# The time mixer's three sums by ones as two products of split operands, the variance sum behind ten weight groups, and affines and state scalings on ScalarE

## The reference, cut to what matters

```python
decay = exp(-DECAY_SCALE * sigmoid(w0 + tanh(wl) @ w_w2))
a = sigmoid(a0 + al @ w_a2)
kk = heads(k * k_k)
kk = kk / maximum(norm(kk, axis=-1), 1e-12)             # sum 1: squares over a head
k = k * (1.0 + (a - 1.0) * k_a)
y = rwkv7_scan(r_h, w_h, k_h, v_h, kk, a_h)
ym = mean(y, axis=-1)
yv = mean(square(y - ym), axis=-1)                      # sum 3: variance over a head
y = (y - ym) * rsqrt(yv + GN_EPS) * gn_g + gn_b
bonus = sum(r_h * k_h * r_k, axis=-1) * v_h             # sum 2
y = (y + bonus) * g
```

## Time and profile before

| | |
|---|---|
| median of 3 runs | 2407.47 us (2406.66 to 2407.55) |
| profiled execution, first to last instruction | 2404.5 us |
| PE busy | 2157.6 us, 90% |
| DVE busy | 1529.0 us, 64% |
| ACT busy | 684.3 us, 28% |
| software DMA queue (gathers) | 53.1% of 16 engines' span |

### The profile page before, as it was taken

How to read it: one execution, slowest core, us unless ns; L and a number is a source line. 1 busy time by engine, 2 the same in 40 slices (tenths; PEclk the granted TensorE clock), 3 DMA queues, 4 the chain that set the end, 5 groups by cost and what they waited for, 6 DMA issues and landing times.

```text
span 2404.5 us, 37848 instructions
## 1 busy us (share of the span) xinstructions
PE 2157.6 (90%) x15331; PEld 1510.5 (63%) x15331; DVE 1529.0 (64%) x2605; ACT 684.3 (28%) x1366; POOL 659.7 (27%) x539
## 2 busy tenths in 40 slices
PE   9999999999999999998999889978877787777776
PEld 8999999999899999987554444433332233222222
DVE  7778888888765455548876567667446444444445
ACT  6555555455344444432121111111011000000000
POOL 1000000000000000004554555555455445444442
PEclk9999999999999999999999999999999999999999
DMA  6533333333367666679999999999999999999997
GB/s 213 141 95 98 102 88 101 103 88 98 106 184 194 185 187 187 190 270 342 417 427 424 425 423 426 427 427 426 427 427 428 426 427 427 427 427 427 427 427 289
DMA packets 348320, 708.19 MB, mean 295 GB/s; under 512 B 13834, under 2 KB 272482, under 8 KB 281826
## 3 DMA queue, kind: packets, MB, share of 16 engines
q0 software_dynamic: 74176, 537.01, 53.1%
q1 hardware_dynamic: 273732, 168.55, 24.1%
q10 hardware_dynamic: 240, 0.22, 0.0%
HBM read 703.63 MB, written 2.10 MB: 294 GB/s over the span
## 4 chain that ended last, share of the span: by engine, by line
DMA 36%; PE 17%; issue 2%; DVE 2%; POOL 1%; DVEq 0%; ACT 0%; POOLq 0%; ACTq 0%
DMA query_w<-in_v_table,experts 17%; DMA rows<-in_v_table,experts 13%; PE bank L1980 7%; PE project L1980 4%; DMA rows<-in_u_table,experts 3%; DMA up_rows<-in_u_table,experts 3%; PE bank L247 2%; DMA down_row_more<-in_v_table,experts 2%; PE bank L1896 2%; PE project L247 1%; PE bank L1938 0%; PE bank L1944 0%; PE bank L1612 0%; PE bank L1923 0%; POOL rows L1851 0%
## 5 line engine op out<-in xcount | busy, mean ns | idle before, releaser
L2102 DVE CUSTOM_DVE_ANT_0 rows<-rows,h 128x2048 f32<-128x2048 f32 x170 | 388.7, 2292 | 329.7 <-DMA rows<-in_u_table,experts 329.5
L1851 POOL DMA_INDIRECT rows<-in_u_table,experts x170 | 182.9, 1076 | 1097.7 <-DVE experts L1449 1040.0
L232 DVE TENSOR_TENSOR w_half_rest<-w_half,w_half_high 128x1024 fp32r<-128x1024 f32 x224 | 271.4, 1219 | 160.5 <-ACT w_half_high L211 160.3
L247 PE MATMUL project<-hT_high,w_half_high 128*128 128x272 f32 (+1 forms) x1152 | 351.1, 305 | 0.4 <-PEq L254 0.3
L1980 PE MATMUL bank<-query_w,merged_spare 128*128 128x512 f32 x608 | 283.6, 602 | 60.7 <-DMA query_w<-in_v_table,experts 47.3
L1980 PE MATMUL bank<-rows,merged_spare 128*128 128x512 f32 x612 | 286.4, 605 | 57.2 <-DMA rows<-in_v_table,experts 43.8
L247 PE MATMUL project<-hT,w_half_high 128*128 128x272 f32 (+1 forms) x1152 | 329.2, 286 | 0.0
L247 PE MATMUL project<-hT_high,w_half_rest 128*128 128x272 f32 (+1 forms) x1152 | 328.7, 285 | 0.0
L2102 DVE CUSTOM_DVE_ANT_0 up_rows<-up_rows,h 128x2048 f32<-128x2048 f32 x86 | 197.0, 2292 | 168.7 <-DMA up_rows<-in_u_table,experts 168.7
L211 ACT CAST w_half_high<-w_half 128x1024 fp32r<-128x1024 f32 x224 | 234.9, 1051 | 204.3 <-PE merge_ps L247 120.6
L1980 PEld LDWEIGHTS bank<-rows,merged_spare 128*128 128x128 f32 x612 | 114.0, 192 | 223.2 <-issue 127.3
(11 more groups left out here) (435 smaller groups left out, 3760.3 us busy)
## 6 DMA issues: line engine op xcount, KB each, us to landing
w_half<-in_w_in SPq DMA_DIRECT2D x176, 512.0 KB, 4.1
w_half<-in_w_branch_a SPq DMA_DIRECT2D x32, 512.0 KB, 3.9
out_w<-in_w_out SPq DMA_DIRECT2D x16, 1024.0 KB, 5.6
w_half<-in_w_branch_b SPq DMA_DIRECT2D x16, 512.0 KB, 3.9
query_w<-in_w_q_peer SPq DMA_DIRECT2D x8, 1024.0 KB, 16.2
out_w<-in_w_q_peer SPq DMA_DIRECT2D x6, 1024.0 KB, 19.1
lora_weights<-in_w_in SPq DMA_DIRECT2D x4, 896.0 KB, 14.1
rows<-in_u_table,experts POOLq DMA_INDIRECT x170, 21.1
```

The source lines that it names most:

```text
L232: return eng.tensor_tensor(low.bitcast(F32R), x, high, ALU.subtract)
L247: mm = nc.tensor.matmul(out, a.bitcast(F32R), b.bitcast(F32R), start=start and n == 0, stop=stop and n == 2)
L1851: pool.indirect_dma_start(ur[n % RU], None, w["u_table"][0], bass.IndirectOffsetOnAxis(ap=k.idx[:, t, h, j:j + 1], axis=0)).then_inc(s_u[n ...
L2102: v.tensor_tensor_reduce(ur[n % RU], ur[n % RU], k.h[:, n // (HEADS * TOPK), :], 1.0, 0.0, ALU.mult, ALU.add, dots(n, n + 1)).then_inc(s_d ...
```

## The change

- The three sums: instead of one f32 matmul, `head_sums` makes two f32r products with a rounded matrix of ones, `ones_high`, one of the high part of the operand and one of its rest. The high parts come from ACT: a second Square for `nm` and for `gv` (`sq_high`, `ysq_high`), a copy `bk` for `bo` (`rk_high`). The rests come from DVE (`kq`, `br`, `gq`, each one `rest_bits`).
- The variance sum `gv` on PE moves from ahead of `f` 10 to behind it. On ACT `gv` moves from ahead of `split` 1 to behind `t` 0.
- `t1` (now `lt`) and the second half of `sg` go from DVE to ACT; `S_decayed` for chunks 1 to 3 goes from DVE (unit `r` there is gone) to ACT, behind the copy of `rhs`; `ends` goes from DVE to ACT (`en`).
- `cv` and the copy to `gcur` are gone: scalars are read from `k.vec`.

```diff
 PE_ORDER
-    ... ("t", 0, 1), ("gv", 0, 3), ("f", 10, 0),
+    ... ("t", 0, 1), ("f", 10, 0), ("gv", 0, 3),
 ACT_ORDER
-    ("u", 2, 3), ("nm", 0, 1), ("r", 3, 3), ("u", 3, 3), ("r", 4, 3), ("split", 5, 0), ("split", 0, -1), ("e", 1, 0),
-    ("u", 4, 3), ("yc", 0, 3), ("yf", 0, 2), ("gv", 0, 3), ("split", 1, -1), ("t", 0, 1), ("t", 1, 1), ("r", 0, 2), ("e", 2, 0),
+    ("u", 2, 3), ("bk", 0, 1), ("nm", 0, 1), ("r", 3, 3), ("u", 3, 3), ("r", 4, 3), ("split", 5, 0), ("split", 0, -1),
+    ("e", 1, 0), ("u", 4, 3), ("yc", 0, 3), ("en", 0, 1), ("yf", 0, 2), ("split", 1, -1), ("t", 0, 1), ("gv", 0, 3), ("t", 1, 1),
...
+            def head_sums(out, high, rest):
+                nc.tensor.matmul(out, ones_high[:].bitcast(F32R), high.bitcast(F32R), start=True, stop=False)
+                return nc.tensor.matmul(out, ones_high[:].bitcast(F32R), rest.bitcast(F32R), start=False, stop=True)
...
-                wait(pe, q["ksq"], p + 1)
-                nc.tensor.matmul(low[:, 0:T], ones, sq[:, real], start=True, stop=True).then_inc(q["norm"], 1)
+                wait(pe, q["ones"], 1)
+                wait(pe, q["ksplit"], p + 1)
+                head_sums(low[:, 0:T], sq_high[:], sq_rest[:, real]).then_inc(q["norm"], 1)
...
+            def bk(_, p, par):
+                wait(act, q["bonus"], p)
+                wait(act, q["rk"], p + 1)
+                nc.scalar.copy(rk_high[:].bitcast(F32R), rk[:, CH:TP]).then_inc(q["rkr"], 1)
+            def lt(_, p, par):
+                wait(act, q["sig"], p * 3 + 2)
+                nc.scalar.activation(t1[:, real], am[:, real], ACT.Identity, scale=k.vec[:, V_KAH, p:p + 1],
+                                     bias=k.vec[:, V_KAC, p:p + 1]).then_inc(q["rate"], 1)
...
             def r_(c, p, par):
                 nc.scalar.copy(rhs[:], rhs_ps).then_inc(q["rhsc"], 1)
+                if 0 < c < NCH - 1:
+                    wait(act, q["S"], p * 4 + c)
+                    nc.scalar.activation(spc[:], s[c % 2][:], ACT.Copy, scale=ends[par][:, c:c + 1]).then_inc(q["spc"], 1)
...
-                nc.scalar.activation(ysq[:], y_ps, ACT.Square).then_inc(q["sqr"], 1)
+                nc.scalar.activation(ysq[:], y_ps, ACT.Square)
+                nc.scalar.activation(ysq_high[:].bitcast(F32R), y_ps, ACT.Square).then_inc(q["sqr"], 1)
...
             def s_(c, p, par):
                 if c < NCH - 1:
-                    d()
+                    wait(dve, q["endc"], p + 1)
+                    if c:
+                        wait(dve, q["spc"], p * 3 + c)
```

More of the change, by code:

```diff
@@ L890, in gv @@
             def gv(_, p, par):
-                wait(pe, q["sqr"], p + 1)
-                nc.tensor.matmul(var_ps, ones, ysq[:], start=True, stop=True).then_inc(q["var"], 1)
+                wait(pe, q["ysplit"], p + 1)
+                head_sums(var_ps, ysq_high[:], ysq_rest[:]).then_inc(q["var"], 1)
             schedule(PE_ORDER, {"f": f, "lw": lw, "la": la, "lg": lg, "nm": nm, "bo": bo, "gr": gr, "rb": rb, "t": t,
@@ L914, in e @@
                 wait(act, k.s_used, p * 6 + 2 * i + 2)
-                nc.scalar.activation(t[:, real], pr[(3 * p + i) % 2][:, 0:T], ACT.Copy, scale=cur[par][:, o:o + 1]).then_inc(q["own"], 1)
+                nc.scalar.activation(t[:, real], pr[(3 * p + i) % 2][:, 0:T], ACT.Copy, scale=k.vec[:, o, p:p + 1]).then_inc(q["own"], 1)
             def kn_(_, p, par):
@@ L919, in kn_ @@
                 wait(act, q["st"], p)
-                nc.scalar.activation(kn[:, real], kx[par][:, real], ACT.Copy, scale=cur[par][:, V_KK:V_KK + 1])
+                nc.scalar.activation(kn[:, real], kx[par][:, real], ACT.Copy, scale=k.vec[:, V_KK, p:p + 1])
             def sq_(_, p, par):
@@ L924, in sq_, with en @@
                 wait(act, q["norm"], p)
-                nc.scalar.activation(sq[:, real], kx[par][:, real], ACT.Square, scale=cur[par][:, V_KK:V_KK + 1]).then_inc(q["ksq"], 1)
+                nc.scalar.activation(sq[:, real], kx[par][:, real], ACT.Square, scale=k.vec[:, V_KK, p:p + 1])
+                nc.scalar.activation(sq_high[:].bitcast(F32R), kx[par][:, real], ACT.Square, scale=k.vec[:, V_KK, p:p + 1]).then_inc(q["ksq"], 1)
+            def bk(_, p, par):
[6 more added lines that the diff above has]
+                                     bias=k.vec[:, V_KAC, p:p + 1]).then_inc(q["rate"], 1)
+            def en(_, p, par):
+                wait(act, q["S"], (p - 1) * 4)
+                wait(act, q["exp1"], p + 1)
+                nc.scalar.copy(ends[par][:], pe_[:, CH - 1::CH]).then_inc(q["endc"], 1)
             def lw(_, p, par):
@@ L929, in lw @@
                 wait(act, q["lora_mm"], p * 3 + 1)
-                nc.scalar.activation(sg[:, real], low[:, 0:T], ACT.Tanh, scale=0.5, bias=cur[par][:, V_W0H:V_W0H + 1]).then_inc(q["sig"], 1)
+                nc.scalar.activation(sg[:, real], low[:, 0:T], ACT.Tanh, scale=0.5, bias=k.vec[:, V_W0H, p:p + 1]).then_inc(q["sig"], 1)
+                wait(act, q["sig"], p * 3 + 1)
+                nc.scalar.activation(sg[:, real], sg[:, real], ACT.Copy, scale=0.5, bias=0.5).then_inc(q["sg"], 1)
             def la(_, p, par):
@@ L934, in la @@
                 wait(act, q["lora_mm"], p * 3 + 2)
[L935 removed]
+                nc.scalar.activation(am[:, real], low[:, 0:T], ACT.Tanh, scale=0.5, bias=k.vec[:, V_A0H, p:p + 1]).then_inc(q["sig"], 1)
             def lg(_, p, par):
@@ L945, in ex @@
                 wait(act, q["csum"], p + 1)
-                nc.scalar.activation(pe_[:, real], cs[:, real], ACT.Exp, scale=-DECAY)
+                nc.scalar.activation(pe_[:, real], cs[:, real], ACT.Exp, scale=-DECAY).then_inc(q["exp1"], 1)
                 nc.scalar.activation(pi[:, real], cs[:, real], ACT.Exp, scale=DECAY)
```

64 lines of the change are left out of this document (32 added, 32 removed), and 16 rows, old and new, of tables (ACT_ORDER, DVE_ORDER, PE_ORDER).

## The result

| | before | after |
|---|---|---|
| median | 2407.51 us | 2415.59 us |
| profiled execution, first to last instruction | 2404.5 us | 2412.4 us |
| PE busy | 2157.6 us | 2157.2 us |
| DVE busy | 1529.0 us | 1518.3 us |
| ACT busy | 684.3 us | 725.7 us |

The account below looks back on a forecast made before the run. PE's unbroken list of work was taken to bound the time mixer; savings on PE and new waits summed to +0.2 us, so 2407.47 became 2407.7 us, with an 8-in-10 range of 2401.1 to 2413.1.

Parts of the forecast that it names:

- `nm` and the chain of chunk 3: PE, `S,A_st` of chunk 2 to `rhs,Y_st` of chunk 3: ACT's queue delays `rhs`, +0.30 us in 13 blocks, +3.9.
- `bo` and `gv`: Two sums on PE, cheaper as f32r products: 0.20 us each saved, -3.0 us over 15 blocks and -2.8 over 14.
- state update on DVE: DVE's work ahead of `S` in the middle: costs and gives nothing, since DVE waits for PE there (0.15 us).
- middle block: One middle block of the time mixer on PE: -0.10 us, as long as before within 0.15 us.
- second block: First block with a pair at stage 1: additions on ACT ahead of the root cost net +0.8 us, ends 0.4 and 1.2.
- third block: Third block of the time mixer: savings of `nm` and `bo` come through, -0.41 us, with no new wait.
- PE's waits for `S` in the last blocks: Last two blocks, where pooling windows delay `S`, and one block with a 0.2 us wait: PE waits less, -0.6 us.
- last pair, hole: Behind the last variance sum: PE starts the next weight half +2.7 us later, waiting some 3.7 us with nothing to do.
- a block as long as before within 0.15 us: Sign that the forecast is right, in the trace after: block length unchanged within 0.15 us.
- the waits for `rhs`: Sign in the trace after: PE waits for `rhs` in chunk 3 in 13 blocks, 0.5 us each, nowhere else in the middle.
- The last sentence of the prediction: Error most feared: a wait on an engine's queue taken as free, each 0.1 us in a block being 1.4 us.
- Rival 2: ACT's additions delay `yaT_high`, so the state update in chunk 1 and third `rhs` come late: 2413.1 us, chance 0.14.

Follow-up runs that it names:

- second pair of profiles: Before and after each run once more, unchanged, for a second trace: 2407.48 us and 2414.53 us, profile spans 2405.4 and 2411.4 us.
- control of before: The kernel before run once more, unchanged, for a second trace: 2407.48 us, ratio 1.0002.
- second profile of after: The changed kernel run once more, unchanged, for a second trace: 2414.53 us, ratio 1.0033.
- the experiment that takes them back: Changed kernel with the wait for `Snew` written first in DVE's state update, `endc` and `spc` behind it: 2411.89 us, ratio 1.0024.
- the cast alone: Kernel before plus an unread 256-column cast on ACT ahead of the table load between `U` of chunk 2 and `rhs` of chunk 3: 2409.54 us, ratio 1.0011.
- one kernel had 14 holes of 2.5 us: Changed kernel with late wait first, table load moved, last pair's halves ahead of the root, but variance sum back ahead of ten weight groups: 2451.62 us, ratio 1.0185.
- Edits that lie on one chain: Changed kernel with late wait first, table load behind `U` of chunk 3, last pair's halves ahead of the root, all together: 2399.64 us, ratio 0.9972.

## Why the prediction was wrong

Against the second pair of profiles, from the first decay product on:

| step | predicted | measured | |
|---|---|---|---|
| `nm` and the chain of chunk 3 | +0.30 a block | +0.35 (5.45 to 5.80 us), and 0.05 behind it | right, a little small |
| `bo` and `gv` | -0.20 each | -0.21, -0.18 | right |
| state update on DVE | 0 | +0.21 a block | **missed** |
| middle block | -0.10 | +0.21 | 13 blocks: 2.8 us longer, 1.3 shorter by the forecast: +4.1 us |
| second block | +0.8 | +0.93 | right size |
| third block | -0.41 | +0.09 | +0.5 |
| PE's waits for `S` in the last blocks | -0.6 | -0.9 (1.2 to 0.3) | right size |
| last pair, hole | 2.72 later | 2.72 later | right |
| half clock behind the hole | none | +1.6, in most profiles | **missed** |

From the first decay product to the start of the merge the second pair differs by 7.1 us, and of the 6.9 us beyond the forecast's 0.2 the three lines that were off make 4.1 + 0.5 + 1.6 = 6.2. I can't assign the last 0.7 to a step. The whole spans differ by 6.0, since the stretch of the merge is 1.3 us longer in the control of before than in the second profile of after, and just as much longer than in the first profile of before: scatter, in work that the change doesn't touch. The medians differ by 7.1 and 8.1.

**The step that failed** is the one on DVE: "In the middle it costs and gives nothing, since DVE waits for PE there ahead of `S`". The idle 0.15 us was read as a margin. But DVE's idle time there is the wait for `Snew` itself: the chain PE, DVE, PE runs right through it, and anything between the arrival of `Snew` and the start of the update is on PE's path. I costed the scaling that left DVE and not the waits that came in its place: 0.21 us a block, 2.6 us by the experiment that takes them back, where the prediction had nothing. This term alone would have made the forecast 2410.3 us; the third block's wait for `B_st` and the half clock behind the hole, both put at nothing too, are the others. Of the signs it named, the one to fail was "a block as long as before within 0.15 us"; the waits for `rhs` came, though each shows as 0.27 us and not 0.5. The last sentence of the prediction names this sort of error, with its price; it looked for it in a queue, and it was in the taking of the wait. Rival 2 had the state late and 2413.1 us, but for another cause: `yaT_rest` doesn't hold the update (in after DVE is idle 0.29 us ahead of `S` of chunk 1). It gets no credit.

**The chain of chunk 3** was right in mechanism and nearly in size. `S_decayed` takes 0.35 us, 0.25 from start to start (492.53 to 492.78 us in after), not 0.30 and 0.20. The Trainium skill's formula, "ScalarE: Activation LUTs", What ACT_TABLE_LOAD costs, which the prediction set at 0.33, lies nearer. Those 0.05 us are the whole difference between +0.30 and +0.35. `bk` takes 0.41 and puts the load 0.30 later, as worked out. That the step behind `rhs` of chunk 3 starts another 0.05 later wasn't in the sum; the cast alone shows the same.

**The last pair** came out to the hundredth. From `RBKT_st,U` to the sum 3.85 us (675.40 to 679.25), to the half 7.83 us (to 683.23), both as predicted from the earlier trace rows. What fails is the sentence behind it: PE has "nothing to do" for 3.6 us, and I didn't ask what state it is in afterwards.

**The third block.** `nm` and `bo` save 0.41 there, as predicted, and the wait for `B_st` that the prediction knew only in the second block turns up and takes it back. After's timeline of PE:

```profile
116.96 0.68 PE L714 MATMUL low_rank<-constants,B_st 64*64 64x64 f32 x16 [0.30 <-DVE B_st L1123]
```

The second block's +0.93 comes by another way than forecast, too: PE waits 0.77 us for `k_square_rest` ahead of the sum itself, where I looked at the root behind it; the wait for `B_st` grows only from 0.76 to 1.0 us.

## What to carry to other kernels

When an operand's producer moves to another engine, count the wait that it adds to the consumer, and, in a program built like this one, write the wait that arrives last first, so that it sits on the instruction: the order of three lines was worth 2.6 us here. Judge a move of work by the queue it joins and not by an engine's busy share: ACT at 28% had 0.1 us of room at the one place where the change used it, and moving two entries of a table gave back 6.6 us. And a saving on PE (8.8 us here) is only seen once no other engine is late; a slower result doesn't say that the saving isn't there.

## What the runs showed of the hardware that I had not expected

- A wait taken by an instruction of its own lets the next one start later than a wait on the instruction: 0.10 us with two more waits (0.60 against 0.50 us from PE's first product to the update), 0.07 with one (0.56 against 0.49), the data being there in each case.
- PE's granted clock fell to 0.50 for some 3.4 us in three profiles and 6.8 us in a fourth, each time within 1.0 us of the end of 3.6 us without work; in a fifth it stayed at 1.00. Where one kernel had 14 holes of 2.5 us, it fell at 8 of them, between 0.7 us before the end of the hole and 0.6 us after it, and at 6 it didn't. Where the idle time was cut to 1.1 or 0.9 us the clock stayed at 1.00. It also fell between 13 and 26 us of the span in ten of the 14 profiles, of unlike kernels, and not in others of the same kernel. Why one execution or one block has it and the next not stays open.
- Edits that lie on one chain add up to more than their parts: 12.4 us one by one, 14.9 against the same control together; the blocks of the profiles show 1.2 us of these 2.5. A late state update was hidden in the wait for `rhs`, and could only be won once that was gone.
